# Rotation tables built beside the second expert loop, and the expert window copied by VectorE

## The reference, cut to what matters

```
y = (silu(xr @ w_gate[e]) * (xr @ w_up[e])) @ w_down[e]     # 32 experts, 3 x 2 MB of weights each
x = rms_norm(x, final_norm)                                 # ends the first block
```

```
proj = rms_norm(x, mix_norm_g) @ w_in                       # 4616 columns: u, q, k, v, o, two gates, 2048 gates
a_bar = exp(lam * dt);  b_bar = (a_bar - 1) / lam * b_mat   # 32 groups x 64 complex states
states[t] = a_bar * states[t-1] + b_bar @ u[t]              # 256 steps
y = (c_mat @ states).real + d * u;  y = gelu(y);  y = y * sigmoid(y @ w_glu + b_glu)
```

## Time and profile before

| what | us |
|---|---|
| median of 3 runs (lowest, highest) | 1881.53 (1880.58, 1883.73) |
| the profiled execution: its time | 1880.79 |
| its span, first to last instruction | 1879.0 |
| busy: PE, DVE, ACT, POOL | 1660.7, 462.0, 234.0, 236.9 |
| mean DMA rate over the span | 268 GB/s |

### The profile page before, as it was taken

How to read it: one execution, slowest core, us unless ns; L and a number is a source line. 1 busy time by engine, 2 the same in 40 slices (tenths; PEclk the granted TensorE clock), 3 DMA queues, 4 the chain that set the end, 5 groups by cost and what they waited for, 6 DMA issues and landing times.

```text
span 1879.0 us, 22392 instructions
## 1 busy us (share of the span) xinstructions
PE 1660.7 (88%) x8945; PEld 1038.3 (55%) x8945; DVE 462.0 (25%) x976; ACT 234.0 (12%) x504; POOL 236.9 (13%) x498
## 2 busy tenths in 40 slices
PE   4799999998989687999899998799788898899998
PEld 3555444444446546554444444586677585488853
DVE  5311111111122322111111111465563202133411
ACT  2011000000021210100000000311211111200000
POOL 2000000000000000000000000089970000000000
PEclk8799999999989788999999999999899898999999
DMA  9299999999994133999999999931223334334410
GB/s 344 104 370 426 427 427 426 426 426 426 428 369 179 45 108 137 418 428 425 425 428 425 427 426 425 342 135 68 90 90 104 142 135 134 101 126 143 147 55 23
DMA packets 104422, 504.05 MB, mean 268 GB/s; under 512 B 16714, under 2 KB 42667, under 8 KB 71595
## 3 DMA queue, kind: packets, MB, share of 16 engines
q1 hardware_dynamic: 90551, 497.21, 65.5%
q10 hardware_dynamic: 13812, 6.05, 1.2%
HBM read 502.19 MB, written 1.05 MB: 268 GB/s over the span
## 4 chain that ended last, share of the span: by engine, by line
PE 49%; DMA 32%; POOL 9%; DVE 5%; issue 3%; ACT 2%; ACTq 0%; POOLq 0%; DVEq 0%
DMA ring<-in_w_up 31%; PE PS L717 11%; PE PS L1172 8%; PE PS L1182 4%; PE PS L1119 3%; PE PS L949 3%; PE PS L760 3%; PE PS L662 2%; PE PS L1109 2%; PE PS L923 1%; PE PS L1100 1%; POOL arena L2227 1%; POOL XN L2223 1%; POOL XN L2226 1%; PE PS L746 1%
## 5 line engine op out<-in xcount | busy, mean ns | idle before, releaser
L717 PE MATMUL PS<-ring,arena 128*64 128x256 f32 x4096 | 469.9, 383 | 77.5 <-DMA ring<-in_w_up 53.6
L717 PEld LDWEIGHTS PS<-ring,arena 128*64 128x64 f32 x4096 | 295.9, 138 | 273.4 <-DMA ring<-in_w_up 74.1
L760 PE MATMUL PS<-ring,arena 128*64 128x512 f32 x1024 | 233.8, 598 | 1.1 <-ACT arena L1315 1.1
L1705 DVE TENSOR_TENSOR arena<-PS,arena 128x256 f32<-128x256 f32 x64 | 27.2, 424 | 803.5 <-ACT arena L1308 803.5
L2172 POOL COPY arena<-arena 128x512 f32 x64 | 60.4, 943 | 859.6 <-DVE arena L1705 797.7
L760 PEld LDWEIGHTS PS<-ring,arena 128*64 128x64 f32 x1024 | 68.2, 136 | 157.7 <-issue 157.7
L1172 PE MATMUL PS<-hT,ring 128*128 128x256 f32 x704 | 153.8, 382 | 1.0 <-issue 1.0
L1172 PEld LDWEIGHTS PS<-hT,ring 128*128 128x128 f32 x704 | 134.9, 192 | 19.9 <-issue 1.3
L746 PE MATMUL PS<-arena 64*128 64x512 f32 x512 | 127.2, 615 | 1.9 <-ACT arena L1324 1.9
L938 PE MATMUL PS<-hT,ring 128*128 128x256 f32 x448 | 100.4, 386 | 0.0
L938 PEld LDWEIGHTS PS<-hT,ring 128*128 128x128 f32 x448 | 86.5, 194 | 12.4 <-issue 0.5
(11 more groups left out here) (374 smaller groups left out, 1503.7 us busy)
## 6 DMA issues: line engine op xcount, KB each, us to landing
ring<-in_w_gate SPq DMA_DIRECT2D x64, 2048.0 KB, 25.5
ring<-in_w_up SPq DMA_DIRECT2D x64, 2048.0 KB, 25.6
ring<-in_w_down SPq DMA_DIRECT2D x64, 2048.0 KB, 24.6
ring<-in_f_w_up SPq DMA_DIRECT2D x22, 1024.0 KB, 7.1
ring<-in_w_in SPq DMA_DIRECT2D x9, 2048.0 KB, 20.2
ring<-in_f_w_down SPq DMA_DIRECT2D x5, 2048.0 KB, 7.8
ring<-in_x_wkv SPq DMA_DIRECT2D x4, 2048.0 KB, 8.0
ring<-in_wo SPq DMA_DIRECT2D x2, 2048.0 KB, 13.3
```

The source lines that it names most:

```text
L717: mm = pe.matmul(PS[half * WINDOW:(half + 1) * WINDOW, bank, m * half_f:(m + 1) * half_f], xw[bank][:, k, :], mat[:, k, half * half_f:(hal ...
L760: mm = pe.matmul(PS[half * WINDOW:(half + 1) * WINDOW, 3, :], hidT[:, w, k * WINDOW:(k + 1) * WINDOW], mat[:, k, half * 512:(half + 1) * 5 ...
```

## The change

Seven things are moved or replaced; what is computed stays the same.

1. The loads. Three small loads (both parts of lam, log dt) are issued by SP at the kernel's start, behind the vectors. The two loads of b (4096 pieces of 64 bytes) are issued by ACT in `loads_ahead` of layer 1. `final_norm` (`gain`), four loads of c, `w_if` and two of `b_if` are issued by SP behind the fifth slab of the mixing stage (`mix_loads`).
2. In the pool stage `router_loads(0)` is issued behind `hT_upper("pool")`, not ahead of it. PE transposes lam and dt there, behind a wait for the three loads and for a small POOL copy; ACT runs its six small activations; DVE takes the reciprocal of |lam|^2 behind a wait for POOL (`s5_th` 2).
3. POOL works out a_bar, the factors of b_bar and the eight powers (`s5_discretise`, some 75 instructions on 128x16) ahead of `moe(0)`.
4. DVE copies the expert windows. The copy of expert e+2 stands behind the product of expert e+1 and ahead of the gates of expert e. `slots`, `gates2` and `gates` move from `arena` to `hT`.
5. POOL builds the whole table E for all eight turns (`s5_tables`, 72 instructions of up to 128x512, and six for b_bar) in one region of `arena`, once the second sort is done; it signals `e_ready` once. ACT waits for that ahead of `norm("first_out")`, since the temporaries lie in XN.
6. In the loop of the mixing stage POOL builds `bpad` and `cblk` alone, and DVE waits for `e_ready` in turn 0 only. ACT's `gate` waits for `states`, since the gates are written over the table.
7. The sixty small DVE instructions, three PE transposes and three ACT activations at the start of the mixing stage are gone.

```diff
             vectors(VEC_PARTS[FIRST_VECTORS:], "vec2_loaded")
+            for at, name in ((0, "s5_lam_re_2"), (32, "s5_lam_im_2")):
+                sp.dma_start(s5_rows[at:at + S5J, :], a[name][0].rearrange("(j g) p -> j (g p)", g=2)).then_inc(s["s5_loaded"], 16)
+            sp.dma_start(ldt2[64:64 + S5J, :], a["s5_log_dt_2"][0].rearrange("(j g) -> j g", g=2)).then_inc(s["s5_loaded"], 16)
...
+            def mix_loads():
+
+                sp.dma_start(gain, a["final_norm"].partition_broadcast(P)).then_inc(s["gain_loaded"], 16)
+                for ri, n in enumerate(("re", "im")):
+                    for d in range(2):
+                        sp.dma_start(c_rows[:, ri, :, d * S5P:(d + 1) * S5P],
+                                     a[f"s5_c_{n}_2"][0].rearrange("(c g) h p -> (g h) c p", c=S5C)).then_inc(s["mix_loaded"], 16)
+                sp.dma_start(w_if, w_in[:, IN_IF:IN_GATE].rearrange("(k p) n -> p k n", p=P)).then_inc(s["mix_loaded"], 16)
+                sp.dma_start(b_if[:, 0:MH], a["m_b_i_2"]).then_inc(s["mix_loaded"], 16)
+                sp.dma_start(b_if[:, MH:], a["m_b_f_2"]).then_inc(s["mix_loaded"], 16)
+
             for i, at in enumerate([512 * j for j in range(5)] + [IN_GATE + 512 * j for j in range(4)]):
                 rows(MIX0 + i, w_in[:, at:at + 512], KD, 512)
+                if i == 4:
+                    mix_loads()
...
             turn_norm("pool")
+            pe.wait_ge(s["s5_loaded"], 16 * 3)
+            pe.wait_ge(s["s5_small"], 1)
+            hT_wait("pool")
+            for i in range(3):
+                r = slice(32 * i, 32 * i + S5J)
+                mm = pe.transpose(PS[:, 5 + i, 0:S5J], s5_rows[r, :], ident[r, r])
+            mm.then_inc(s["s5_turned"], 1)
...
             norm("pool")
-            router_loads(0)
             act.wait_ge(s["vec_ready"], 1)
             act.wait_ge(s["pool_step"], 1)
             hT_upper("pool", ["pool_norm"], dsts=[hp[:, :, POOL_PAD:]])
-
...
+            router_loads(0)
+
+            act.wait_ge(s["s5_turned"], 1)
+            act.activation(lre, PS[:, 5, 0:S5J], ACT.Copy)
+            act.activation(lim, PS[:, 6, 0:S5J], ACT.Copy)
+            act.activation(dt, PS[:, 7, 0:S5J], ACT.Exp).then_inc(s["s5_dt"], 1)
+            act.wait_ge(s["s5_th"], 1)
+            act.activation(rad, xdt, ACT.Exp)
+            act.activation(sh, th, ACT.Sin, scale=0.5)
+            act.activation(s1, th, ACT.Sin).then_inc(s["s5_sin"], 1)
+
+            def s5_b_loads():
+
...
+                    act.dma_start(b_in[:, ri], a[f"s5_b_{n}_2"][0].rearrange("(j g) p h -> (g p) j h", g=2)).then_inc(s["s5_loaded"], 16)
...
                     if layer == 0:
                         router_loads(1)
                     else:
-                        act.dma_start(gain, a["final_norm"].partition_broadcast(P)).then_inc(s["gain_loaded"], 16)
+                        s5_b_loads()
...
+                act.wait_ge(s["e_ready"], 1)
                 norm("first_out", ready=4 * TT)
...
                 def gate(i):
                     j = i - MIX_SLABS.index("g0")
+
+                    act.wait_ge(s["states"], j + 1)
 
...
             dve.wait_ge(s["pool_biased"], TT)
+            dve.wait_ge(s["s5_th"], 2)
+            dve.reciprocal(den, den).then_inc(s["s5_small"], 1)
...
+                def sorted_wait(half):
+                    dve.wait_ge(s["sorted_dve"], KD // 2 * (2 * q + half + 1))
+                    dve.wait_ge(s["sorted_act"], KD // 2 * (2 * q + half + 1))
+
                 sorted_out(0)
                 dve.wait_ge(s["route_done"], q + 1)
+                dve.wait_ge(s["pad_ready"], q + 1)
+                sorted_wait(0)
 
                 def experts(windows):
...
+                    def window(e, w):
+
+                        if isinstance(e[0], int) and linear(e, windows, w) == 2:
+                            sorted_wait(1)
+                        if isinstance(e[0], int) and linear(e, 1, 0) >= EXPERTS:
+                            return
+                        start = dve.value_load(starts[0:1, bass.ds(linear(e, 1, 0), 1)], min_val=0, max_val=SLOTS)
+                        dve.tensor_copy(xw[(e[1] * windows + w) % 2], xs[:, :, bass.ds(start + w * WINDOW, WINDOW)])\
+                           .then_inc(g["window"], 1)
...
                             if not last:
                                 hids(next_expert(e), w)
+                                window(*after(next_expert(e), w))
                             window_gates(e, w)
 
+                    window((0, 0), 0)
+                    window(*after((0, 0), 0))
                     for w in range(windows):
                         hids((0, 0), w)
+                        if w:
+                            window(*after((0, 0), w))
...
-                    e_re, e_im = turns[q % 2][:, 0], turns[q % 2][:, 1]
+                    e_re, e_im = E[:, q, 0], E[:, q, 1]
                     u_re, u_im = (PS[:, 4 + ri, :].rearrange("p (j n) -> p j n", j=2) for ri in range(2))
                     z_re, z_im, r1, r2 = z[:, 0], z[:, 1], rot[:, 0], rot[:, 1]
-                    dve.wait_ge(s["e_ready"], q + 1)
+                    if q == 0:
+                        dve.wait_ge(s["e_ready"], 1)
                     dve.wait_ge(s["bu_mm"], q + 1)
...
-            pool.tensor_tensor(pool_b, pool_b, pool_scale, ALU.mult).then_inc(s["pool_step"], 1)
-            pool.wait_ge(s["pool_step"], 2)
+            step(pool.tensor_tensor(pool_b, pool_b, pool_scale, ALU.mult))
+            pool.wait_ge(s["s5_loaded"], 16 * 3)
+            pool.tensor_copy(s5_rows[64:64 + S5J, :].rearrange("j (g p) -> j g p", g=2),
+                             ldt2[64:64 + S5J, :, None].to_broadcast([S5J, 2, S5P])).then_inc(s["s5_small"], 1)
+            pool.wait_ge(s["s5_small"], 1)
             pool.wait_ge(s["norm_xn"], TT)
...
+            def s5_discretise():
+
+                pool.wait_ge(s["s5_dt"], 1)
+                pool.tensor_tensor(xdt, lre, dt, ALU.mult)
+                step(pool.tensor_tensor(th, lim, dt, ALU.mult))
+
+                step(pool.tensor_scalar(kq, th, 1.0 / (2 * math.pi), None, ALU.mult))
+                step(pool.tensor_scalar(kq, kq, 12582912.0, None, ALU.add))
+                step(pool.tensor_scalar(kq, kq, 12582912.0, None, ALU.subtract))
+                for part in (6.28125, 0.0019350051879882812, 3.019915981956753e-07):
+                    step(pool.tensor_scalar(ta, kq, part, None, ALU.mult))
+                    step(pool.tensor_tensor(th, th, ta, ALU.subtract))
+                pool.tensor_scalar(th, th, 3.1415925, -3.1415925, ALU.min, ALU.max).then_inc(s["s5_th"], 1)
+                pool.tensor_tensor(ta, lre, lre, ALU.mult)
+                step(pool.tensor_tensor(tb, lim, lim, ALU.mult))
+                pool.tensor_tensor(den, ta, tb, ALU.add).then_inc(s["s5_th"], 1)
+                pool.wait_ge(s["s5_sin"], 1)
+
+                step(pool.tensor_tensor(cmn, sh, sh, ALU.mult))
+                step(pool.tensor_scalar(cmn, cmn, -2.0, None, ALU.mult))
+                pool.tensor_scalar(c1, cmn, 1.0, None, ALU.add)
+                pool.tensor_tensor(ta, rad, cmn, ALU.mult)
+                pool.tensor_scalar(tb, rad, 1.0, None, ALU.subtract)
+                step(pool.tensor_tensor(aim, rad, s1, ALU.mult))
+                step(pool.tensor_tensor(are, ta, tb, ALU.add))
+
+                pool.wait_ge(s["s5_small"], 2)
...
+                pool.tensor_copy(wre[:, 0, :], c1)
+                step(pool.tensor_copy(wim[:, 0, :], s1))
...
+            def s5_tables():
+
+                pool.wait_ge(s["sorted_mm"], KD // 2 * 4)
+                pool.wait_ge(s["slots_spread"], 2)
+                pool.memset(E[:, :, 0, :, 0:1], 1.0)
+                step(pool.memset(E[:, :, 1, :, 0:1], 0.0))
+                for k in range(8):
+                    n = 1 << k
+                    m = min(S5J // 2, 256 // n)
+                    f_re, f_im = (w[:, k, :].rearrange("p (q j) -> p q j", j=2) for w in (wre, wim))
+                    tmp = [XNf[:, 512 * i:512 * i + 2 * m * n].rearrange("p (q j n) -> p q j n", q=m, j=2) for i in range(4)]
+                    for q in range(0, S5J // 2, m):
+                        qs = slice(q, q + m)
+                        e_re, e_im = E[:, qs, 0], E[:, qs, 1]
+                        g_re, g_im = (f[:, qs, :, None].to_broadcast([P, m, 2, n]) for f in (f_re, f_im))
+                        pool.tensor_tensor(tmp[0], e_re[:, :, :, 0:n], g_re, ALU.mult)
+                        pool.tensor_tensor(tmp[1], e_im[:, :, :, 0:n], g_im, ALU.mult)
+                        pool.tensor_tensor(tmp[2], e_re[:, :, :, 0:n], g_im, ALU.mult)
+                        step(pool.tensor_tensor(tmp[3], e_im[:, :, :, 0:n], g_re, ALU.mult))
+                        pool.tensor_tensor(e_re[:, :, :, n:2 * n], tmp[0], tmp[1], ALU.subtract)
+                        step(pool.tensor_tensor(e_im[:, :, :, n:2 * n], tmp[2], tmp[3], ALU.add))
```

(20 more changed lines are left out.)

221 lines of the change are left out of this document (58 added, 163 removed).

## The result

The changed kernel took 1889.13 us (median of 6 runs, 1884.57 to 1893.62) against 1881.49 us (6 runs, 1878.91 to 1883.73) for the kernel before: a ratio of 1.0046, 95% interval 1.0029 to 1.0063. It is slower by 0.3 to 0.6%. The forecast was 1884.0 with a range of 1875 to 1892 and 0.37 for slower.

What follows compares the result with a forecast made beforehand. Bound by TensorE and DMA, in the scan by GpSimd's table. Terms -16.4 (scan) + 16.4 (`gain`) - 0.2 + 2.1 + 0.4 + 0.2 = +2.5 us on 1881.5 gave 1884.0; range 1875 to 1892.

Steps and rivals of the forecast that it cites:

- The scan loop: Mixing stage's scan: with the table out of the turns, PE sets the pace and the last rotation begins 16.4 us earlier.
- `gain` behind five slabs: Start of mixing stage: `gain` lands behind five w_in slabs on SP's queue, so X is scaled 16.4 us later.
- The term for the transposes: Ahead of slab "u": the three PE transposes that go save 0.2 us.
- The loads of b: Loop 1: 4096 small pieces cost the saturated stream 3.4 us, `gain` leaving gives back 1.2; +2.1 us.
- The pool stage and loop 0's entry: Before loop 0: later router loads -0.9, wait for GpSimd +0.8, reciprocal and short blocks +0.5; entries +0.2 for both loops.
- The pad memset: Routing of loop 0: GpSimd's 1.8 us memset behind `s5_discretise` ends before the first window copy; 0, at worst +7 us.
- A: Start of mixing stage: `gain` lands early, by overtaking or an earlier fifth slab; the 16.4 us wait goes, 1867.6; 10%.
- B: PE's wait ahead of the c transposes: small loads behind `gain` land last, at 1228.3; +6.3 us, 1890.3; 10%.
- C: Pool stage: GpSimd's 15 instructions at the crowded price end at 37.5, pad memset 1 us late; +3, 1887; 8%.
- D: Scan turns 4 and 5: exponents and ACT, or the clock, take half the scan's gain; +8 us, 1892; 7%.
- E: Scan turn 5: the shorter wait no longer lowers the clock, so the scan gives 3 to 5 us more; 1880; 10%.
- F: Start of mixing stage: the table is not ready at 1192 and ACT waits; 1%.

Runs made afterwards that it cites:

- second pair: Unchanged copies of the changed kernel and of the kernel before, each profiled a second time: spans 1884.6 and 1878.2 us.
- `reciprocal_late`: Changed kernel with DVE's wait for `s5_th` 2 and the reciprocal moved behind the eight additions to X: 1886.07 us, ratio 1.0026 to the kernel before.
- `gain_early`: Changed kernel with the load of `final_norm` alone issued ahead of the third w_in slab: 1880.20 us, ratio 0.9999 to the kernel before.
- `gain_on_scalar`: Changed kernel with early small loads, late reciprocal, pad on DVE, b loaded in attention, and `final_norm` on ACT's queue: 1866.56 us, ratio 0.9932 to the kernel before.
- the two comparisons: Changed kernel and an unchanged copy of it, each timed against the kernel before: ratios 1.0046 and 1.0029.

## Why the prediction was right or wrong

- **The bound now**: right. Taking the tables out of the turns gave what the chain said, and PE took over.
- **The scan loop, -16.4**: right, -17.5 (one profile of each: -16.1). Turns 17.6 us apart, one wait of 4.3 us (5.4 forecast), its multiplication again at the slow clock (3.78 us). From turn 2's multiplication to the last rotation it took 1408.23 - 1306.66 = 101.6 us, where the layout had 1380.0 - 1277.19 = 102.8. The size is in part luck. From turn 2 on the gain was 17.7 us in these two profiles, 1.2 more than laid out, and slab "u", which ran in part at the slow clock behind the long wait (15.50 us instead of 13.98), gave 1.5 back. The tail didn't hang on as before either: PE now waited 4.3 us for the last rotation, not 1.7, and made the eight matmuls behind it at a granted clock of 0.50. They took 1.5 us longer in these profiles and 0.4 in the second pair, which covers the +0.7 of the table's last row. PE's rows in the kernel before and in the changed one:

```profile
1407.11 1.99 PE L984 MATMUL PS<-arena 128*128 128x256 f32 x8 [1.71 <-DVE arena L2017]
```

```profile
1418.93 3.54 PE L1005 MATMUL PS<-arena 128*128 128x256 f32 x8 [4.30 <-DVE arena L2006]
```

- **`gain` behind five slabs, +16.4**: right in mechanism, order and size (+17.7). The issue was forecast 23.1 us behind last up and came 22.4 behind it. The rest, 1.3 us, is a later landing. The term for the transposes, -0.2, was wrong in sign: +0.75. The transposes of X ran at the slow clock before (3.64 us) and after (3.67). The eight transposes of c behind them took 1.94 us at a granted clock of 0.50, where the kernel before had 1.09 at 1.00; in `reciprocal_late` they took 1.07 at 1.00, and the stretch was 10.8 us again.
- **The small loads behind it**: right that they were hidden; `gain_early` shows them 10 us deep behind `gain`.
- **The loads of b, +2.1**: 443.7 - 442.1 = +1.6 over all profiles. Two errors met: 3.4 us for the packets was too much (1.8), and the 1.2 us given back for `gain` were not there. The page "DMA: Bandwidth & Descriptors" of the Trainium skill (Specifications, at least 512 bytes a piece for line rate) is borne out in its direction; the estimate made from it, 4.9 us for these loads, was nearly three times the measured 1.8. What the step didn't ask is how long the issue holds ACT.
- **The pool stage and loop 0's entry, +0.4 and +0.1**: wrong, and the miss of the forecast. It came to +5.0. Four pieces failed. The 0.9 us that the later router loads free were counted as won, though GpSimd's new work beside the additions took them back; I had written that the contention is there "before and after alike". `s5_th` 2 came at 36.1, not 35. The entry of loop 0 cost 0.5 us. And I priced a delay of PE at its own length: removing the wait of 1.8 us (and the collision that the earlier routing would have met) gave 3.1 at the loop's end, since the sort and the first gate matmuls ran longer at the slow clock. The bounds, -1 to +4, left out what stood at their edge.
- **The pad memset**: forecast free, and it was, by 0.3 us: DVE's copy in the changed kernel began 53.91, and the memset had ended at 53.63. The rule that the prediction took from the Trainium skill, page "SBUF — State Buffer", section Who interferes with whom, is what `reciprocal_late` ran into: a VectorE copy in two-port mode and a GpSimd instruction exclude each other for the whole instruction. The trace agrees, 1.80 us in the place of 0.17. I had looked for it in the loop, where it held up five copies by up to 1.1 us under cover, and not in the routing.
- **Rivals**: A (0.10) didn't happen, and `gain_on_scalar` shows what it would have taken. B's depth was right, its decision point wasn't reached. C (0.08) is what happened in the pool stage, at some 60% of its lateness (36.1 against 34.2, where it had 37.5), and its 1887 lies nearest to the mean of the two comparisons (+6.5 us, so 1888.0 beside a median of 1881.5); B's 1890.3 lies nearer to the 1889.13 of the result, by a mechanism that didn't act. The second half of C, a late memset, did not happen. C deserved more than 0.08: it needed only a price for one instruction that the crowded row already showed. D, E and F did not happen.
- **The signs given beforehand**: the wait for `final_norm`, the single wait in turn 5 and the 17.6 us between turns came. Slab "u" began 28.0 and 24.8 us later in the two pairs of profiles, not 16 to 20, and last up of loop 1 came 9.5 and 6.3 us later, not 2 to 3. The sign set for a pool stage gone wrong, a wait of DVE for GpSimd of over 2 us, didn't fire: it was 1.79.

With the terms as measured, 5.0 + 1.4 + 17.7 + 0.75 - 17.5 + 0.7 = +8.1 us (the stretch between the loops left out as chance), beside +7.6 and +5.3 of the two comparisons. The forecast of +2.5 had the two large terms right; the pool stage and the entry of loop 0 are what it lacked.

## What to carry to other kernels

When work is moved off a critical engine, list what its data had to give way to: here the tables took the room in which `gain` waited, and the load that was pushed behind 10 MB on a full queue cost all that the move had won. A load that is wanted soon belongs ahead of the bulk on its queue, or on a queue of its own. A wait put into a stage without slack can cost more than its length where the clock is low behind it (the wait was 1.8 us and its repair gave 3.1 here), and a stage that is made earlier has to be looked at for what it then runs beside.

## What the runs showed of the hardware that was not expected

- A load of 0.5 MB on a second queue landed in 6.4 us; on the queue of the w_in slabs the same load took 15.8 and 16.8 us.
- SP was held 27.43 us by four issues of 2 MB, and ACT 15.60 us by one load of 2048 pieces of 64 bytes behind three like it, and 4.18 us by one behind a single other. Issues that stood alone cost 0.3 to 0.4 us in the same kernels; right behind others, that price doesn't hold.
- A DVE copy of 8 elements a partition took 1.80 us instead of 0.17 beside a memset of GpSimd, and a copy of an expert window 1.50 instead of 0.43 beside an operation of its table.
- A branch into the loop was followed by 0.42 us without work on GpSimd and by 2.76 us on DVE. The traces don't show why.
- The same kernel's router matmuls took 3.7 us in one execution and 6.25 in another, and the stretch between the loops differed by 3 to 6 us. One profile can't carry a difference of a few microseconds.
